# The head of a two-layer hybrid encoder: adaLN weights alone on SyncE's queue, state-space steps between their products, and the products in two column halves of the array

## The reference

```
for layer in (0, 1):
    mod = c @ w_ada[layer] + b_ada[layer]            # c: one vector per sequence, w_ada: 1024 x 3072
    shift, scale, gate = split(mod, 3)
    h = rms_norm(x, norm_g[layer]) * (1 + scale) + shift
    if layer == 0:
        q, k, v, g_a, u, g_s = split(h @ w_in_even)   # widths 512,128,128,512,512,512
        o_a = sliding-window attention with rope (8 heads, 2 kv heads, chunks of 64, window 128)
        o_s = gelu(S5 state-space scan of u + d*u), then a GLU with w_glu
        out = concat(o_a*silu(g_a), o_s*silu(g_s)) @ w_out_even
    else:
        b_g, c_g, hv, g_c = split(h @ w_in_odd)       # 4 x 1024
        out = (silu(g_c) * b_g * short_conv(c_g*hv)) @ w_out_odd
    x = x + gate * out
y = rms_norm(x, final_g)
```

## Time and profile before

| | |
|---|---|
| median of 3 runs | 2302.28 us |
| the profiled execution's own time | 2302.61 us |
| its span in the trace | 2300.7 us |
| TensorE busy | 2161.7 us, 94% |
| mean granted TensorE clock | 0.952 of full |
| DMA | 414.95 MB, mean 180 GB/s |
| first full dense run of TensorE | from about 160 us |

### The profile page before, as it was taken

One profiled execution on the slowest core, in us unless ns is written; L12 is line 12 of the kernel. 1 busy time (PEld: TensorE's weight loads), 2 busy tenths in 40 slices (PEclk: granted clock), 3 DMA queues, 4 the chain that ended last, 5 costly groups with the idle time before them and its releaser, 6 DMA issues.

```text
span 2300.7 us, 27036 instructions
## 1 busy us (share of the span) xinstructions
PE 2161.7 (94%) x11026; PEld 1680.6 (73%) x11026; DVE 814.2 (35%) x1506; ACT 497.6 (22%) x1030; POOL 452.4 (20%) x319
## 2 busy tenths in 40 slices
PE   7778799899999999999999999999998989999996
PEld 2237676688888757888888677888897767788885
DVE  7332453334434452212435613113251542422222
ACT  1132253332221431100213311002112421200010
POOL 0032722465432201010104010111032001100011
PEclk9879899999999999999999999999978979999998
DMA  7776642698778514655575145554733203344431
GB/s 282 232 258 236 236 157 82 242 322 290 262 282 259 187 62 162 219 194 190 183 250 208 65 165 189 194 188 178 203 147 109 93 33 114 112 145 146 147 129 61
DMA packets 86273, 414.95 MB, mean 180 GB/s; under 512 B 12405, under 2 KB 13461, under 8 KB 51893
## 3 DMA queue, kind: packets, MB, share of 16 engines
q1 hardware_dynamic: 80688, 402.66, 50.0%
q10 hardware_dynamic: 5460, 10.55, 1.9%
HBM read 323.51 MB, written 86.33 MB: 178 GB/s over the span
## 4 chain that ended last, share of the span: by engine, by line
PE 86%; DVE 5%; DMA 2%; POOL 2%; issue 1%; ACT 1%; SPq 1%; DVEq 0%; ACTq 0%; POOLq 0%
PE bank L680 21%; PE bank L681 20%; PE bank L682 20%; PE bank L941 5%; PE bank L701 2%; PE bank L629 2%; PE bank L700 2%; PE bank L899 2%; PE bank L900 2%; PE bank L817 1%; PE bank L775 1%; PE bank L880 1%; PE bank L805 1%; DMA ring<-in_dense 1%; PE bank L748 1%
## 5 line engine op out<-in xcount | busy, mean ns | idle before, releaser
L680 PE MATMUL bank<-p_hh,pair 128*128 128x512 f32 x1952 | 785.4, 402 | 28.8 <-POOL pair L447 15.4
L681 PE MATMUL bank<-p_hl,pair 128*128 128x512 f32 x1952 | 773.9, 396 | 0.0
L682 PE MATMUL bank<-p_hh,pair 128*128 128x512 f32 x1952 | 773.1, 396 | 0.0
L680 PEld LDWEIGHTS bank<-p_hh,pair 128*128 128x128 f32 x1952 | 373.2, 191 | 127.6 <-POOL pair L447 17.8
L682 PEld LDWEIGHTS bank<-p_hh,pair 128*128 128x128 f32 x1952 | 372.5, 191 | 83.4
L681 PEld LDWEIGHTS bank<-p_hl,pair 128*128 128x128 f32 x1952 | 372.9, 191 | 80.0 <-issue 1.4
L447 POOL TENSOR_TENSOR pair<-ring,pair 128x1024 fp32r<-128x1024 f32 x66 | 164.7, 2498 | 210.7 <-ACT pair L438 210.7
L1259 POOL TENSOR_TENSOR pp_mem<-pp_mem 128x512 f32<-128x512 f32 x48 | 62.1, 1295 | 623.4 <-ACT pp_mem L1025 623.4
L1348 POOL TENSOR_TENSOR p_g<-p_t,pp_mem 128x512 f32<-128x512 f32 x32 | 41.4, 1292 | 575.9 <-DVE p_t L1802 575.9
L1678 DVE SCALAR_TENSOR_TENSOR p_x<-bank,mod,p_x 128x512 f32<-128x512 f32 x64 | 47.4, 750 | 261.1 <-PE bank L682 261.1
L1776 DVE TENSOR_TENSOR pp_mem<-p_sw,bank 128x512 f32<-128x512 f32 x32 | 22.0, 689 | 308.9 <-PE bank L682 308.7
(11 more groups left out here) (303 smaller groups left out, 2452.0 us busy)
## 6 DMA issues: line engine op xcount, KB each, us to landing
pair<-parts_scratch SPq DMA_DIRECT2D x198, 1024.0 KB, 4.8
parts_scratch<-pair SPq DMA_DIRECT2D x66, 1024.0 KB, 7.5
ring<-in_dense SPq DMA_DIRECT2D x66, 512.0 KB, 5.3
pair<-ssm_scratch SPq DMA_DIRECT2D x24, 1024.0 KB, 7.2
ring<-in_ada SPq DMA_DIRECT2D x24, 512.0 KB, 4.6
p_H<-in_ada SPq DMA_DIRECT2D x24, 512.0 KB, 4.8
p_x<-in_x SPq DMA_DIRECT2D x4, 2048.0 KB, 25.5
pair<-glu_scratch SPq DMA_DIRECT2D x8, 1024.0 KB, 4.9
```

Of the source, the lines that this page charges most:

```text
L680: pe.matmul(o, ah, bh, start=first, stop=False)
L681: pe.matmul(o, ah, bl, start=False, stop=False)
L682: return pe.matmul(o, al, bh, start=False, stop=last)
```

## The change

What it does, edit by edit:
1. **Products.** The two matmuls of a chunk go to different output partitions, k = 0 to 0:2 and k = 1 to 64:66 (`HD * k`). ScalarE copies both (24 copies instead of 12), into four row buffers outside the rope buffer, and `ada_turn` sums the two while turning: 8 matmuls with two float32 records each instead of 4 transposes.
2. **Order on TensorE.** 44 chunks in one loop, a B step after each of chunks 19 to 26, a Toeplitz step after each of chunks 27 to 34; the last 4 chunks and two turns follow the norm's column sums.
3. **Queues.** SyncE issues nothing but adaLN chunks until i = 42. The stores `scratch[0]` and `scratch[2]`, the 8 Toeplitz moves and x of block 1 are issued by ScalarE between its copies. x now goes to `prompt.g`, behind the first move, so it waits for two stores and not for the moves. ScalarE copies row 8 behind the first move and x, and row 9 behind the fifth.
4. **Early weights.** u0 to u3 are loaded raw into four free slots of `pp_mem` (two at i = 42, two after the last adaLN chunk); ScalarE splits u0 and u1 before `prep_done`, GpSimd forms their remainders before it too; `ring` is free for k and v.
5. **`load_x(1)`** moves from behind u1 to ahead of (xr0, xi0), with a wait for the scratch stores.
6. **`open_bank`** is gone, 8 per block and stream (40 in all: 8 in each block for the prompt, 8 for the sample in block 4).
7. `prep_done` is reached with two signals (GpSimd's and VectorE's) instead of three; SyncE's is gone.

```diff
+NEARLY = 4
...
+        B_STEPS, C_STEPS = 19, 27
...
+    def source(self, blk, l):
+        return self.g if self.prompt and blk == 0 else self.norm[l][0]
+        def raw(n):
+            if n < NEARLY:
+                return pp_mem[:, n * SLOT:(n + 1) * SLOT]
+            return ring[:, (n - NEARLY) % NRAW, :]
...
         @block.sync
...
             for i in range(2, NADA):
                 s = i % NADASLOT
-                if i == 20:
-                    sp.wait_ge(prep_free, 8)
-                    sp.dma_start(scratch[0], xin_stage).then_inc(scratch_out, 16)
-                elif i == 28:
...
-                elif i == 41:
-                    sp.dma_start(scratch[1], intra_stage).then_inc(scratch_out, 16)
+                if i == 42:
                     sp.wait_ge(dve_built, TOEPLITZ)
+                    load_early(range(2))
                 if i >= NADASLOT:
                     sp.wait_ge(ada_used, i - NADASLOT + 1)
                 sp.dma_start(ada_slots[s], w_ada[i]).then_inc(raw_in[s], 16)
+            load_early(range(2, NEARLY))
+            sp.wait_ge(kt_moved, 16 * L)
+            sp.dma_start(scratch[1], intra_stage).then_inc(scratch_out, 16)
             for i in range(4):
                 sp.dma_start(glu_scratch[i], w_dense[DENSE.index(f"glu{i}")]).then_inc(kt_moved, 16)
...
             for i, held in enumerate(PAIRS + [None] * 3):
+                if held == ("xr0", "xi0"):
+                    sp.wait_ge(scratch_out, 48)
+                    load_x(1)
...
                 if held == "u1":
                     sp.wait_ge(ada_turned, NROW)
                     load_rope(1)
-                    load_x(1)
...
         @block.tensor
...
+            def ada_chunk(i):
+                j = i // 4
+                pe.wait_ge(raw_in[i % NADASLOT], 16 * (i // NADASLOT + 1))
+                for k in range(2):
+                    mm = pe.matmul(psum[2 + j % 2][HD * k:HD * k + 2, :], c_in[:, 2 * (i % 4) + k, :],
+                                   ada_slots[i % NADASLOT][:, 512 * k:512 * k + 512],
+                                   start=(i % 4 == 0), stop=(i % 4 == 3))
+                mm.then_inc(ada_used, 1)
+            def ada_turn(j):
+                pe.wait_ge(ada_rows, 2 * j + 2)
+                for m in range(4):
+                    at = 2 * (4 * j + m)
+                    for k in range(2):
+                        mm = pe.matmul(psum[5][:, at:at + 2], ada_row[2 * (j % 2) + k][:, m * P:(m + 1) * P],
+                                       ident[0:2, 0:2], start=(k == 0), stop=(k == 1))
+                mm.then_inc(ada_turned, 1)
+            for i in range(NADA - 4):
+                ada_chunk(i)
+                if i == 3:
+                    pe.wait_ge(const_loaded, NCONST)
+                if i % 4 == 3 and i > 4:
+                    ada_turn(i // 4 - 1)
+                if B_STEPS <= i < B_STEPS + 8:
+                    b_powers(i - B_STEPS)
+                elif C_STEPS <= i < C_STEPS + 8:
+                    toeplitz_rows(i - C_STEPS)
...
-                        open_bank(o)
...
+            norm_sums(sample, 1, 0)
             norm_sums(prompt, 0, 0)
-            norm_sums(sample, 1, 0)
-            ada_product(NROW)
+            for i in range(NADA - 4, NADA):
+                ada_chunk(i)
+            for j in range(NROW - 2, NROW):
+                ada_turn(j)
...
         @block.scalar
...
+            for i in range(32):
+                if i % 4 == 3:
+                    copy_rows((i // 4,))
+                if B_STEPS <= i < B_STEPS + 8:
+                    n = i - B_STEPS
+                    act.wait_ge(prep_full, n + 1)
...
+                    if n == 7:
+                        act.wait_ge(prep_free, 8)
+                        act.dma_start(scratch[0], xin_stage).then_inc(scratch_out, 16)
+                elif C_STEPS <= i:
...
+            act.wait_ge(dve_built, C_MATRIX)
+            act.dma_start(scratch[2], cout_stage).then_inc(scratch_out, 16)
+            for n in range(32 - C_STEPS, 8):
+                act.wait_ge(prep_full, 9 + n)
...
+            act.wait_ge(dve_built, TOEPLITZ)
+            act.wait_ge(filled, 8)
+            for j in range(L):
+                act.dma_start(intra_stage[CH * j:CH * j + CH, :, CH * j:P], kt_rows[:, :, 0:P - CH * j])\
+                    .then_inc(kt_moved, 16)
+                if j == 0:
+                    act.wait_ge(scratch_out, 32)
+                    act.dma_start(prompt.g[:, :, :], xs[0][:, :, 0:TB]).then_inc(prompt.sem["x_early"], 16)
+                    copy_rows((8,))
+                if j == 4:
+                    copy_rows((9,))
...
             square(sample, 1, 0)
-            square(prompt, 0, 0, range(4))
-            copy_rows((10,))
-            square(prompt, 0, 0, range(4, KT))
-            copy_rows((11,))
-            act.wait_ge(prep_done, 3)
-            act.wait_ge(scratch_out, 48)
+            square(prompt, 0, 0)
             for name in ("u0", "u1"):
                 split_hi(act, 1, name, streams_of)
+            copy_rows((10, 11))
+            act.wait_ge(prep_done, 2)
             shift(prompt, 0, 0)
```

More of the change, by code:

```diff
@@ L393, in loads_before @@
             s, k = place(blk, name)
-            return sum(by_dma(*((n * NPAIR + s) // len(PAIRS) + 1, (n * NPAIR + s) % len(PAIRS))) for n in range(k))
+            return int(s < NEARLY) + sum(by_dma(*((n * NPAIR + s) // len(PAIRS) + 1, (n * NPAIR + s) % len(PAIRS)))
+                           for n in range(k))
         def wait_pair(eng, blk, name):
@@ L446, in split_lo @@
             hi, lo = parts(blk, name)
-            pool.tensor_tensor(lo, ring[:, n % NRAW, :], hi.bitcast(F32), ALU.subtract).then_inc(split, 1)
+            pool.tensor_tensor(lo, raw(n), hi.bitcast(F32), ALU.subtract).then_inc(split, 1)
         def ut(S, t):
@@ L472, in encoder @@
         d_in = prompt.st[0:CH, :, :].rearrange("p a b -> p (a b)")[:, 0:GROUPS]
-        ada_row = prompt.rope[0:2, :, :]
+        ada_row = [prompt.rope[0:2, 0, :], prompt.rope[0:2, 1, :], prompt.kT[0:2, 0:TB],
+                   prompt.v[0:2, 0:4, :].rearrange("p t n -> p (t n)")]
         mask_in = u_rows[:, :, :].rearrange("p a b -> p (a b)")[:, 0:P + 1024]
@@ L622, in _, with b_powers @@
             c_in = v("c").rearrange("p (k s) -> p k s", k=KT)
[L624 to L649, removed]
+            def ada_chunk(i):
[14 more added lines that the diff above has]
+                mm.then_inc(ada_turned, 1)
+            def b_powers(n):
+                if n == 0:
+                    pe.wait_ge(dve_built, B_POWERS)
                 if n >= 2:
@@ L657, in _, with toeplitz_rows @@
                 mm2.then_inc(prep_full, 1)
[L658 to L662, removed]
+            def toeplitz_rows(n):
+                if n == 0:
+                    pe.wait_ge(dve_built, C_POWERS)
                 pe.wait_ge(prep_free, 7 + n)
@@ L673, in _ @@
                 mm2.then_inc(prep_full, 1)
-            for j in range(6, NROW):
-                ada_product(j)
+            pe.wait_ge(vec_loaded, 16)
+            for i in range(NADA - 4):
[8 more added lines that the diff above has]
+                    toeplitz_rows(i - C_STEPS)
             def three(o, stationary, moving, first, last):
@@ L733, in tokens @@
                 return S.h_mem[:, at:at + P], S.h_mem[:, at + S.N:at + S.N + P]
-            def open_bank(o):
-                pe.matmul(o[:, 0:1], ident[:, :], ones[:, 0:1], start=True, stop=True)
             def norm_sums(S, blk, l):
@@ L1008, in _ @@
                     .then_inc(prep_free, 1)
[L1009 removed]
+            act.wait_ge(dve_built, TOEPLITZ)
[9 more added lines that the diff above has]
+                    copy_rows((9,))
             def square(S, b, l, ks=range(KT)):
[L1012 removed]
+                x, sq = S.source(b, l), S.norm[l][1]
                 for k in ks:
@@ L1513, in scale @@
             def scale(S, b, l, k):
-                x, sq = S.norm[l][:2]
+                x, sq = S.source(b, l), S.norm[l][1]
                 if k < KT:
```

68 lines of the change are left out of this document (31 added, 37 removed).

## The result

The changed kernel takes 2313.42 us (median of 7 runs, 2296.57 to 2320.2), the kernel before 2298.18 us (7 runs on the same chip): ratio 1.0058, 95% interval 1.0041 to 1.0076, some 13 us slower where 29.8 us less were forecast. Its profiled execution took 2313.03 us. The seven runs lie wide apart: the one of 2296.57 us had a mean granted clock of 0.943, the other six 0.932 to 0.934.

The account below looks back on a forecast made before the run. TensorE, 94% busy, was taken to bound the kernel, with the gain in the head before the first dense product. Head 25.1 us, block 1 -3, open_bank 7.7: 29.8 us off 2302.61, 2272.8 us; range 2260 to 2290.

Parts of the forecast that it names:

- Price of a chunk and of a turn: Head, adaLN products in halves: 0.94 us per chunk instead of 1.72, and 1.9 us per eight-matmul turn.
- rival A: Head, adaLN chunks: halves overlap only in part, 1.3 us per chunk, 2278 us in all; chance 0.15.
- B: Head, adaLN chunks: the halves do not overlap, a chunk stays at 1.72 us, 2293 us in all; chance 0.09.
- C: Head: each change of half or shape drains the array, 2.06 us per chunk, 2309 us in all; chance 0.06.
- Chunks 4 to 19 and B steps: Head: 1.5 us per chunk, chunk 19's turn done at 39.8; B steps then take 12.9 us, to 53.0.
- Toeplitz steps: Head: eight steps with chunks and a turn between take 22.5 us, to 82.2; the add ends at 83.5.
- Rival D: Moved transfers cost more: ScalarE held 6 us, block 1 loses 6, half clock costs Toeplitz steps 3; 2285 us; chance 0.12.
- ScalarE's queue: Head: moves 14.4 us, x, four row copies and a 3 us hold (bounds 0 and 6); ScalarE free at 104.
- Norm, last row, start of the dense work: End of the head: squares to 116.6, column sums to 118.7, mod and gscale to 129.0, first dense matmul 133.8.
- Block 1: x ahead of the weight loads costs 5 us, earlier k and v return 2.5; cost 3 us, bounds -3 and +6.
- open_bank: Dropping 40 matmuls of 0.31 us: 6.2 us before yt, 1.5 before block 4's ut; gain 7.7, bounds 5 and 10.

Follow-up runs that it names:

- e1: Changed kernel with adaLN products, copies and turns back in one half of the array: 2302.17 us, ratio 1.0013 to the kernel before.
- e4: Kernel before with only the products, copies and turns put in halves, order and queues as before: 2305.26 us, ratio 1.0019.
- e11: Changed kernel with chunks 0 to 26 multiplied twice in halves, first into a bank nobody reads: 2327.56 us, ratio 1.0123 to the kernel before.
- e2: Changed kernel with the eight Toeplitz steps together behind chunk 27, products still in halves: 2305.87 us, ratio 1.0022 to the kernel before.
- e3: Changed kernel with the eight Toeplitz moves issued by SyncE behind its last adaLN load: 2298.01 us, ratio 0.9981 to the kernel before.
- e8: The kernel of e7 with x of block 1 loaded by SyncE behind u1 again: 2287.34 us, ratio 0.9944 to the kernel before.
- e5: Kernel before without its 40 open_bank matmuls and nothing else changed: 2298.79 us, ratio 1.0005.
- e7: The kernel of e6 with open_bank back at its two places: 2287.94 us, ratio 0.9954 to the kernel before.
- e6: Changed kernel with whole products and old turns, Toeplitz steps together, moves on SyncE after its adaLN loads, no open_bank: 2286.10 us, ratio 0.9946 to the kernel before.
- e10: The kernel of e6 with open_bank only in block 4 and for the sample: 2300.26 us in its one run.

## Why the prediction was wrong, by its steps

Against the profiled execution the forecast was 2272.8, measured were 2313.03, 40.2 us more. Where they arose:

| stretch | forecast | measured | off by |
|---|---|---|---|
| end of the Toeplitz add | 83.5 | 106.2 | +22.7 |
| ScalarE's moves, x and copies | 20.5 | 27.9 | +7.4 |
| squares to end of column sums | 14.7 | 16.3 | +1.6 |
| last chunks, turns, mod, to the dense start | 15.1 | 14.2 | -0.9 |
| dense start to the first GLU, against before | +1.8 | +2.1 | +0.3 |
| first GLU to the end, against before | -6.5 | +2.7 | +9.2 |

(Of open_bank's 7.7 us, 1.2 are counted in block 1, 6.5 behind it.)

- **Price of a chunk and of a turn: right.** 0.96 us against 0.94, 2.0 against 1.9. The halves overlap, rivals A, B and C are out. The Trainium skill, TensorE: Matmul & The Clock Gate, part 3, says that matmuls are strict FIFO, from which rival A worked out 1.3 us per chunk; the four records of 45.38, over after 0.96, disagree.
- **Chunks 4 to 19 and B steps: about right.** Chunk 3 ended at 15.9, not 13.9, and a chunk then took 1.69 us instead of 1.5, so row 3's turn ends at 44.8, not 39.8; the B steps took 13.3 against 12.9. With that the store of scratch[0] lands later: the C-matrix copy is at 69.15, not 62. It did not matter, since VectorE then waited 16.64 us for the last Toeplitz copy.
- **Toeplitz steps: the step that failed.** Counted with 22.5 us at full clock, ending at 82.2, they took 44 at half clock, 60.9 to 104.8. Rival D had put half clock at 3 us and only because of the pause before them; there was no such pause (60.60, then 60.89). The forecast took the chunk's price from `attend`, but not what a long stretch of such work does to the clock. e1 and e4 show from both sides that the halves, with the longer turns they need, bring it down; e11 excludes idle time ahead of the steps. e2 shows that the interleaving multiplies the damage: chunk, turn and step all paid double between the first step and the last, on the path to the add. The Trainium skill, TensorE: Matmul & The Clock Gate, part 1, "What's actually happening", says that "activity releases the throttle"; the earlier trace rows fit that, the stretch 80 to 100 here, without a gap and at 0.50, does not.
- **ScalarE's queue: the hold was seen, but mis-sized, and its weight missed.** The prediction gave the hold behind x 3 us with a bound of 6. One issue alone took 11.24 us, three others 7.96, and the total was 27.9. That it was x in front that made them slow is not shown: in e2 x stood in the same place and all eight moves were issued in 12.7 us. The point is not the 7.4 us over: moves on ScalarE stand in front of the squares whatever they cost. e3 removes them and gains 18 us, more than the halves' clock. The old place on SyncE cost 14.4 us and was called the fault of the head; on ScalarE it cost more.
- **Norm, last row, start of the dense work: right** within 2 us. The column sums ran at half clock (3.58 instead of the 2.1 counted).
- **Block 1: right.** q2's split came 58.8 us after the first dense matmul, 54.6 before, so 4.2 later where 3 were forecast. The wait for the state-space inputs grew from 7.3 to 14.39, but less of the rest was waited for: 2.1 us dearer up to the GLU in all. e8 prices the load's place at nothing.
- **open_bank: a gain of 7.7 us counted, none found.** e5 was no faster than before, and e7, with them back, no slower than e6. From the first GLU to the third, kernels without them take 1.1 to 3.6 us less than the kernel before (4 banks of yt each would be 2.4; the spread of profiles is as large). But the fourth block's v product falls to half clock: 9.7 us more to intra 4 in the changed kernel, 4.8 back behind it. The prediction costed the instructions and not their effect on the clock.

What stays open: why the clock falls. In all five kernels with products in halves ahead of the first Toeplitz step (the changed one, e2, e3, e4, e11) it fell within 2 us of that step and stayed down for the rest of them (e2, e3 and e11 had held it from 40 us on, the changed one from 41, e4 only from 60); with whole products it held through the same steps, interleaved or not. A kernel with products in halves and short turns, or whole products and long turns, was not run. Why single-column matmuls in blocks 1 to 3 keep the clock of v in block 4 up was not isolated either. That a shift of the whole program in time does it is unlikely: the first GLU starts anywhere from 335 to 377 us in the eight kernels without them, and v is at half clock in all eight. Nor was open_bank put back in the changed kernel by itself.

## What to carry to other kernels

Putting products into the two halves of the array can shorten each of them and still lose, if other small work behind it then runs at half clock: read the granted clock of the stretch in a first profile before counting with a price taken from another place. Transfers that an engine issues belong behind the work that others wait for, or on a queue with nothing behind them: here one issue on ScalarE's queue took 0.69 us and another of the same kind 11.24. When a head is put together from several edits, time each alone: here undoing three of them gave 8 to 18 us each, and what was left of the change was 12 us faster than before.

## What the runs showed of the hardware that was not expected

- TensorE busy for 20.00 of 20 us at a granted clock of 0.50 (80 to 100 us; half clock from 61.5 to about 112), and again in v of block 4 (1666 to 1686, 0.50). The same v product with the same instructions had 1.00 in the kernel before (1650 to 1670).
- Where in the program a half-clock stretch falls depends on work hundreds of microseconds earlier: 24 matmuls of one column in blocks 1 to 3 took 12 us out of a stretch in block 4 (466.2 to 453.9 from GLU 3 to intra 4), and with the same kind in block 4 alone it was 472.5 (one run).
- A DMA issue on ScalarE's queue took 11.24 us when a 2 MB load and five moves were in front of it. The issues of the eight moves took 13.7 to 18.0 us on SyncE (e5, e10), and on ScalarE with x among them 12.7 (e2) to 26.4 (e11).
